# A mixture of experts on gathered token lists instead of all tokens, in a float32 two-block transformer kernel

## What is computed

```python
def moe(h, router_w, router_bias, w1, w3, w2):      # 16 experts, 4 groups of 4, D_EXPERT = 512
    scores = jax.nn.sigmoid(t.astype(f) @ router_w.astype(f))
    sel = scores + router_bias.astype(f)
    ...                                             # best group, then the top 2 experts inside it
    gate = ...                                      # (256, 16), two nonzero entries in each row
    for e in range(N_EXPERTS):
        hid = jax.nn.silu(t @ w1[e]) * (t @ w3[e])
        out = out + gate[:, e:e + 1] * (hid @ w2[e])
```

## Time and profile before

| | us |
|---|---|
| median of 3 runs | 1855.85 (1852.56 to 1878.67) |
| the profiled execution | 1855.94 |
| its span, first to last instruction | 1854.2 |
| w1(0) begins (end of the router's logits) | 622 |
| w2(0) ends | 672.7 |
| w2(14) ends, w3(15) begins | 1160.6 |
| last row of the experts' results added (L2320) | 1193.0 |

### The profile page before, as it was taken

How to read it: one execution, slowest core, us unless ns; L and a number is a source line. 1 busy time by engine, 2 the same in 40 slices (tenths; PEclk the granted TensorE clock), 3 DMA queues, 4 the chain that set the end, 5 groups by cost and what they waited for, 6 DMA issues and landing times.

```text
span 1854.2 us, 26650 instructions
## 1 busy us (share of the span) xinstructions
PE 1703.8 (92%) x11424; PEld 1485.0 (80%) x11424; DVE 1035.7 (56%) x1201; ACT 757.6 (41%) x851; POOL 191.4 (10%) x242
## 2 busy tenths in 40 slices
PE   4899988976797899999999999999999989999997
PEld 2678765765696798999999999777999977799996
DVE  1648356565666556555545555756555565655455
ACT  3433233622332343333333334454543365543444
POOL 0013551312320000610000000001000000000000
PEclk8999998976698899999999999999999999999999
DMA  9667500103336344555555555452555544245551
GB/s 351 239 246 242 111 28 1 24 10 81 90 125 219 113 171 166 188 183 183 190 182 182 182 182 182 144 182 76 182 183 191 194 159 162 99 161 196 188 182 68
DMA packets 150174, 289.15 MB, mean 156 GB/s; under 512 B 32439, under 2 KB 35646, under 8 KB 150057
## 3 DMA queue, kind: packets, MB, share of 16 engines
q1 hardware_dynamic: 135304, 270.50, 41.7%
q0 software_dynamic: 4816, 13.41, 2.4%
q10 hardware_dynamic: 9936, 3.54, 0.7%
HBM read 281.07 MB, written 6.37 MB: 155 GB/s over the span
## 4 chain that ended last, share of the span: by engine, by line
PE 77%; DVE 7%; issue 5%; ACT 4%; DMA 2%; DVEq 1%; SPq 1%; ACTq 1%; POOL 0%; POOLq 0%
PE psum L214 23%; PE psum L215 22%; PE psum L216 22%; DVE w_low L184 1%; DMA modw<-in_mod_w_dram 1%; DMA raw<-in_w_out_dram 1%; ACT w_high L179 1%; PE psum L748 1%; DVE w_low L202 1%; PE psum L3067 1%; PE psum L1537 1%; PE psum L765 1%; DVE blk L1173 1%; DVE outer L1170 1%; PE psum L3043 1%
## 5 line engine op out<-in xcount | busy, mean ns | idle before, releaser
L184 DVE TENSOR_TENSOR w_low<-raw,w_high 128x4096 fp32r<-128x4096 f32 x105 | 464.8, 4428 | 321.4 <-ACT w_high L179 319.5
L179 ACT ACTIVATE w_high<-raw 128x4096 fp32r<-128x4096 f32 x107 | 386.6, 3615 | 280.6 <-DMA raw<-in_moe_w_dram 142.5
L214 PE MATMUL psum<-act_high,w_high 128*128 128x256 f32 (+1 forms) x1176 | 337.2, 287 | 5.5 <-DVE w_low L184 5.5
L215 PE MATMUL psum<-act_low,w_high 128*128 128x256 f32 (+1 forms) x1176 | 336.4, 286 | 0.0
L216 PE MATMUL psum<-act_high,w_low 128*128 128x256 f32 (+1 forms) x1176 | 336.3, 286 | 0.0
L214 PEld LDWEIGHTS psum<-act_high,w_high 128*128 128x128 f32 x1176 | 227.6, 194 | 11.1 <-issue 9.6
L215 PEld LDWEIGHTS psum<-act_low,w_high 128*128 128x128 f32 x1176 | 227.5, 193 | 1.2
L216 PEld LDWEIGHTS psum<-act_high,w_low 128*128 128x128 f32 x1176 | 227.6, 194 | 0.7
L216 PE MATMUL psum<-actA_high,w_low 128*128 128x256 f32 x512 | 144.9, 283 | 0.0
L215 PE MATMUL psum<-actA_low,w_high 128*128 128x256 f32 x512 | 144.9, 283 | 0.0
L214 PE MATMUL psum<-actA_high,w_high 128*128 128x256 f32 x512 | 144.8, 283 | 0.0
(11 more groups left out here) (502 smaller groups left out, 3017.9 us busy)
## 6 DMA issues: line engine op xcount, KB each, us to landing
raw<-in_moe_w_dram SPq DMA_DIRECT2D x48, 2048.0 KB, 8.3
raw<-in_w_in_dram SPq DMA_DIRECT2D x20, 2048.0 KB, 8.9
raw<-in_w_up_dram SPq DMA_DIRECT2D x16, 2048.0 KB, 8.7
raw<-in_w_down_dram SPq DMA_DIRECT2D x16, 2048.0 KB, 7.8
modw<-in_mod_w_dram SPq DMA_DIRECT2D x12, 2048.0 KB, 12.8
raw<-in_w_out_dram SPq DMA_DIRECT2D x6, 2048.0 KB, 8.7
raw<-in_w_gate_dram SPq DMA_DIRECT2D x4, 2048.0 KB, 7.9
gates_d<-gstage ACTq DMA_DIRECT2D x8, 256.0 KB, 5.8
```

The costliest lines, as they stand in the source:

```text
L179: act.activation(WH[n % NSLOT][:, 0:elems], RAW[n % NSLOT][:, 0:elems], ACT.Copy).then_inc(s_wh, 1)
L184: dve.tensor_tensor(WL[n % NSLOT][:, 0:elems], RAW[n % NSLOT][:, 0:elems], WH[n % NSLOT][:, 0:elems].bitcast(F32), ALU.subtract).then_inc( ...
L214: pe.matmul(o, aH, wH, start=start, stop=False)
L215: pe.matmul(o, aH, wL, start=False, stop=False)
```

## The change

Experts 0 and 15 stay dense, on all 256 tokens. Experts 1 to 14 run on a list of at most 128 tokens each (128 slots). Three more passes (15, 16, 17) take the tokens past slot 128 of whatever experts are over-full; they always run, with weights fetched by row index. Pass 18 is expert 15. That makes 17 sparse and 2 dense passes in place of 16 dense ones. 57 panels are used instead of 48.

In a sparse pass the gathered tokens are the stationary operand and the panel's 512 columns are streamed: 24 matmuls of 512 columns for each of w1, w3 and w2. The hidden values come out by token, and are scaled by the gate of the slot, turned by 4 transposes (`hid_turn`), and split. The result of a pass, 128 x 1024, is copied out of PSUM by ACT and written to `y_rows` in DRAM by a DMA that ACT issues. The tokens of pass i+2 are gathered by an indirect DMA of POOL, turned by 8 transposes (`chosen_turn`) and split (`chosen_scalar`, `chosen_vector`).

Before the first sparse pass, DVE works out each token's two slots (`slots_vector`, 17 small instructions), from counts that TensorE makes (`positions_tensor`); POOL scatters token numbers and gates into `slots_d` (4 indirect DMAs), loads it back as `table`, and gathers. At the end POOL gathers each token's two result rows (4 indirect DMAs), adds them, and DVE multiplies and adds into `xres` (`pairs_vector`). Panels are handed to ACT, DVE and TensorE whole (`panel_half` waits for the whole panel). The small constants of this (`route_const_pool`) are made by POOL during the merge; `band` and `cmask` are made in passes 5 to 11. Renamed semaphores are left out of the diff.

```diff
+    def slots_vector(dve):
+        ...
+        dve.wait_ge(t_pos, n_pos + 1)
+        ...
+        dve.drain().then_inc(t_slot, 1)
+    def moe_pool(pool):
+        pool.wait_ge(t_slot, n_slot + 1)
+        pool.wait_ge(t_zero, n_zero + 32)
+        for q in range(2 * NT):
+            pool.indirect_dma_start(
+                out=slots_d[:, :], out_offset=bass.IndirectOffsetOnAxis(ap=slot_i[:, q:q + 1], axis=0),
+                in_=entry[:, q, :], in_offset=None).then_inc(t_out, 16)
+        pool.wait_ge(t_out, n_out + 32 * NT)
+        pool.dma_start(table[:, :, :], slots_d[0:REST, :].rearrange("(b s) c -> s b c", s=P)).then_inc(t_in, 16)
+        pool.wait_ge(t_in, n_in + 16)
+        pool.wait_ge(t_rows, n_rows + 16)
+        for i in range(1, LAST):
+            chosen_in(pool, i)
+            ...
+            if spills(i - 1):
+                spill_panel(pool, n_w3(i - 1), "moe_w3", i - 1)
+                spill_panel(pool, n_w1(i), "moe_w1", i)
+                spill_panel(pool, n_w2(i - 1), "moe_w2", i - 1)
+        ...
     def moe_scalar(act):
+        for i in range(1, LAST):
+            act.wait_ge(M["g"], i + 1)
+            act.activation(part_of(sg, i), psum[:, 0, :], ACT.Silu).then_inc(M["silu"], 1)
+            if i == 1:
+                chosen_scalar(act, 2)
+            split_high(act, n_w1(i + 1))
+            split_high(act, n_w2(i))
+            act.wait_ge(t_hT, n_hT + i)
+            act.activation(part_of(hidH, i), psum[:, 6, :], ACT.Copy).then_inc(M["hH2"], 1)
+            split_high(act, n_w3(i + 1))
+            act.wait_ge(s_wdone, n_w2(i) + 1)
+            if i >= 2:
+                act.wait_ge(t_yout, n_yout + 16 * (i - 1))
+            act.activation(ysb[:, :], psum[:, 4:6, :].rearrange("p b n -> p (b n)"), ACT.Copy).then_inc(t_y, 1)
+            act.wait_ge(t_y, n_y + i)
+            act.dma_start(y_rows[P * (i - 1):P * i, :], ysb[:, :]).then_inc(t_yout, 16)
+            if i + 2 < LAST:
+                chosen_scalar(act, i + 2)
     def moe_vector(dve):
+        for i in range(1, LAST):
+            split_low(dve, n_w1(i + 1))
+            dve.wait_ge(s_wdone, n_w3(i) + 1)
+            dve.wait_ge(M["silu"], i + 1)
+            dve.scalar_tensor_tensor(out=part_of(hidf, i), in0=psum[:, 1, :], scalar=table[:, i - 1, 1:2],
+                                     in1=part_of(sg, i), op0=ALU.mult, op1=ALU.mult).then_inc(M["hid"], 1)
+            dve.wait_ge(M["hH2"], i + 1)
+            dve.tensor_tensor(part_of(hidL, i), psum[:, 6, :], part_of(hidH, i).bitcast(F32), ALU.subtract
                               ).then_inc(M["hL2"], 1)
+            split_low(dve, n_w2(i))
+            split_low(dve, n_w3(i + 1))
+            if i + 2 < LAST:
+                chosen_vector(dve, i + 2)
     def moe_tensor(pe):
+        for i in range(1, LAST):
+            chosen_up(pe, 1, n_w3(i), i, 0)
+            chosen_up(pe, 1, n_w3(i), i, 1).then_inc(s_wdone, 1)
+            pe.wait_ge(M["silu"], i + 1)
+            if i + 1 < LAST:
+                pe.wait_ge(t_xL, n_xL + i + 1)
+                chosen_up(pe, 0, n_w1(i + 1), i + 1, 0)
+                hid_turn(pe, i)
+                chosen_up(pe, 0, n_w1(i + 1), i + 1, 1).then_inc(M["g"], 1)
+            ...
+            pe.drain().then_inc(s_wdone, 1)
+            chosen_down(pe, i)
+            if i + 2 < LAST:
+                chosen_turn(pe, i + 2)
```

More of the change, by code:

```diff
@@ L1821, in two_block_kernel @@
     gate = rtr.take("gate", [P, NT, E])
+    c2_end = free_off + 51 * KB + 512 + 13216
     scoT = rtr.take("scoT", [E, T])
-    n2st = stat[:, 64:80]
+    mem = rtr.take("mem", [P, NT, E])
+    slot = rtr.take("slot", [P, NT, E])
+    spill = rtr.take("spill", [P, NT, E - 2])
+    before = rtr.take("before", [P, E - 2, E - 2])
+    full = rtr.take("full", [P, E - 2])
+    nth_full = rtr.take("nth_full", [P, E - 2])
+    shift = rtr.take("shift", [P, E - 2])
+    own = Region(free_off + 51 * KB - 448, 960)
@@ new lines, in moe_sync, with chosen_in @@
+        load_panel(sp, n_w2(0), moe_src("moe_w2", 0))
+        load_panel(sp, n_w1(1), moe_src("moe_w1", 1))
+        for i in range(1, NS):
+            if not spills(i):
+                load_panel(sp, n_w3(i), moe_src("moe_w3", i))
+            if i < LAST and not spills(i + 1):
+                load_panel(sp, n_w1(i + 1), moe_src("moe_w1", i + 1))
+            if not spills(i):
+                load_panel(sp, n_w2(i), moe_src("moe_w2", i))
+    def chosen_in(pool, i):
+        if i >= 2:
+            pool.wait_ge(t_xT, n_xT + i - 1)
+        pool.indirect_dma_start(
+            out=chosen[:, :], out_offset=None, in_=h_rows[:, :],
+            in_offset=bass.IndirectOffsetOnAxis(ap=table[:, i - 1, 0:1].bitcast(I32), axis=0)
+        ).then_inc(t_chosen, 16)
@@ L2286, in moe_vector @@
         dve.drain()
-        dve.wait_ge(M["silu"], E)
+        split_low(dve, n_w2(LAST))
+        dve.wait_ge(M["silu"], NS)
         for b in range(2):
@@ L2299, in moe_vector @@
         dve.wait_ge(B["gcol"], 1)
+        pairs_vector(dve, 0)
         last_vector(dve, 0, 0)
@@ L2304, in moe_vector @@
         turn_vector(dve, 0, 0, 0, 1)
+        pairs_vector(dve, 1)
         last_vector(dve, 1, 0)
@@ new lines, in positions_tensor @@
+    def positions_tensor(pe):
+        pe.wait_ge(t_mem, n_mem + 1)
+        pe.wait_ge(t_const, n_const + 1)
+        o = psum[:, 6, 64:64 + (NT + 1) * E].rearrange("p (t e) -> p t e", e=E)
+        for t in range(NT):
+            pe.matmul(o[:, t, :], earlier[:, :], mem[:, t, :], start=True, stop=t == 0)
+            if t:
+                pe.matmul(o[:, t, :], ones[:, :], mem[:, 0, :], start=False, stop=True)
+        for t in range(NT):
+            m = pe.matmul(o[:, NT, :], ones[:, :], mem[:, t, :], start=t == 0, stop=t == NT - 1)
+        m.then_inc(t_pos, 1)
```

535 lines of the change are left out of this document (382 added, 153 removed).

## The result

| | before | changed |
|---|---|---|
| median | 1854.2 us (4 runs) | 1908.8 us (4 runs, 1904.6 to 1913.3) |
| ratio to before | | 1.026, 95% interval 1.018 to 1.035 |
| profiled execution, span | 1854.2 us | 1911.5 us |
| mean granted clock of it | 0.951 | 0.900 |

The changed kernel is slower by 2.6%. The interval runs from 1.8% to 3.5%: the loss is sure, that it is over 2% only likely.

What follows compares the result with a forecast made beforehand. It took TensorE's matmul stream to bound the kernel before, and a serial chain of copies plus clock falls after. Terms +20.8, +2.5, +4 and +2 made +29.3 on 1854.2, so 1885 us forecast; range 1829 to 1922.

Steps and rivals of the forecast that it cites:

- the sum: Whole kernel: +20.8 + 2.5 + 4 + 2 = +29.3 us on a span of 1854.2 us, giving 1883.5.
- What bounds after the change: Sparse passes: the serial chain through the engines' in-order lists, 26.0 us a pass at full clock, TensorE idle twice.
- The forecast chain: One pass, from w1's first matmul: w2 starts at 9.24 us, the next w1 at 26.07, each step awaiting the last.
- The clock: Both TensorE waits of a pass: falls to 1.2 GHz cost 1.75 us each, making the pass 29.5 us.
- clock stays high: Rival: no fall in one or both waits of a pass, 28 us less for each, 1857 or 1829 us; chance 0.23.
- longer stretches: Rival: low clock costs 2.7 us at each wait, pass 31.4 us, +30 us, 1915 us; chance 0.20.
- The start: Before the first sparse pass: slots, scatters, table, gather and transposes let w1(1) start at 671 us, bounds 666 and 681.
- Constants and overflow panels: Pass 1's reciprocal with its minima, +2.5 us; the nine spill panels fetched through POOL, +2 us (0 to 15).
- 20.8: Start and passes: w2(17) ends at 1181.4 us where w2(14) ended at 1160.6 before, +20.8 us.
- The end: After the last list: gathers, additions and write, about 19 us, hidden under 23 us of expert 15; `pairs_vector` adds +4.
- The second block: Stage after the experts: the forecast had no term for it.
- the forecast's count: TensorE in the expert passes: 17 sparse passes would take 306 us where the 14 rounds take 488.

Runs made afterwards that it cites:

- e4_two_passes_less: Changed kernel with two of its three overflow passes left out: 1857.9 us, distance from hid to hid 30.12 us.
- e7_block2_and_sum: Changed kernel with token-pair sums on VectorE and identity turns in idle times of the second block's attention stage, both layers: 1900.6 us.
- e12_three_halves_filled: e11_three_halves plus 3 filler matmuls ahead of hid's turn and 6 behind it: ratio 0.955 to the kernel before, 1770 to 1775 us in three of six executions.
- e5_hid_first: Changed kernel reordered: hid made before w1's low part, turned before w1, copied before w2's high part: 1852.1 us, distance 26.25 us.
- e9_halves: Changed kernel with w1 and w2 panels split and handed over in two halves: 1851.4 us, distance 25.34 us.
- e11_three_halves: e10 with w3's panel also split and handed over in two halves: 1781.3 us, ratio 0.961 to the kernel before.
- e10: Changed kernel with the edits of e5_hid_first, e9_halves and e7_block2_and_sum together: 1807.7 us, ratio 0.974 to the kernel before.

## Why the prediction came out as it did

The time lay in the range given, 1829 to 1922, and the sign of the forecast was right; 24 us of the 55 were missing, and the forecast's own narrower range, 1865 to 1900, was passed. That the time lies in the range is owed to its width: over half of the missing time came from a stage that the sum does not have. By its own steps:

- **What bounds after the change: right.** The forecast chain has w2 at 9.24 us and w1 at 26.07 us behind the start of w1; at full clock a pass measured 26.12. TensorE's two idle times were put at 4.6 and 3.1 us and are 4.78 and 3.08. Each handoff named is in the rows above, in that order.
- **The clock: right that it falls at both waits in every pass, term too small.** Twice 1.75 was 3.5 us; w1 lost 2.2 and w2 1.9 in the mean, filling the waits gave back 3.9, and the changed kernel ran at 30.06 us where 29.5 was forecast, 9 us over the 16 distances. The rival "clock stays high" fell; 30.06 lies between my value and the 31.4 us of "longer stretches". The Trainium skill ("TensorE: Matmul & The Clock Gate", HAM oscillation in real kernels) describes a fall in every tile where the wait is longer than the tile's matmuls. Here the waits, 4.8 and 3.1 us, were shorter than the 15 and 7.5 us of matmuls ahead of them, and the clock fell all the same, behind both waits of every pass.
- **The start: right in sum, not in its parts.** The slots stood at 643.5, as forecast once it is allowed for that the front of this trace is 3.8 us earlier (both choices stand at 636.4 and not at 640.2). w1(1) began at 668.3 where 671 - 3.8 = 667.2 was forecast. The four scatters took 10.1 us to the table's load (7 forecast), the table 4.5 (7.5), the gather 6.5 (5).
- **Constants and overflow panels: one small, one too large.** The first two distances were 4.7 and 1.8 us over the rest; +2.5 was forecast for the reciprocal. The overflow passes cost nothing over others (e4_two_passes_less), +2 was forecast. With the clock these make w2 of the last list end 32.7 us later than before, where 20.8 + 2.5 + 2 = 25.3 was the sum. That the difference is only 7.4 is in part luck: the front was 3.8 us earlier, which no term had.
- **The end: mis-sized, +10.3 instead of +4.** Write, four gathers and a sum were put at about 19 us and hidden under expert 15. From the last copy of a list's result (1193.6) to the first sum used (1219.4) they took 25.8: 9.0 to the write's landing, 6.2 to issue the gathers, 8.1 to their landing, 2.5 for the sum. The step that failed is the durations. They came from transfers of the kernel before; here two panels of the next stage were loading at the same time (11.2 us to landing), but whether that is what made these longer was not tried.
- **The second block: not in the sum at all, +14.4.** This is the largest miss. I had looked at idle times only where the change made them. The stage has idle times of 0.95 us in the kernel before as well, and the clock stood there; in the changed kernel it fell in the same stage at the same idle time, in both layers (7 us each). e7_block2_and_sum and the four other variants with its turns show that it was this, and that 13 short turns in each layer prevent it.

7.4 + 6.3 + 14.4 = 28.1 us is the difference between +29.3 and +57.3 in the spans.

That the change is no gain although it takes 182 us of TensorE's work away (488 - 306, the forecast's count) has thus two named reasons: the matmuls were the cover of 24 us of copies, and a path of short pieces with idle times between them runs at the lower clock. Both could be mended without touching what is computed (e12_three_halves_filled, some 135 us less than the changed kernel).

Open: why the one pass in which the panels change from SyncE's queue to GpSimd's is 30 us long in e12_three_halves_filled and 35.9 in e5_hid_first. A high part waits 8.4 us for a landing there, in a kernel whose loads land in 10.4 in the median; whether it is the queues' order or the indirect transfers' rate was not tried.

## What to carry to other kernels

When the work that covers the copies is cut, list the copies in the order of each engine's list before anything else: the new time is the chain through them, and an instruction of 0.7 us behind one of 4.4 (hid behind w1's low part) was part of an order that cost 4.5 us of 30. Hand large operands over in parts once nothing covers the hand-over; here halves were worth 4.7 us of 30. Count the clock with every idle time, over many passes and not from one, also in stages that the change does not touch, and give idle TensorE harmless work only where it stands in front of nothing.

## What the hardware showed that I had not expected

- The same code with the same idle time, and two outcomes. Ahead of the probabilities' turn in the attention stage TensorE was idle 0.95 us before, 0.94 in the changed kernel and 0.94 in e9_halves, which does not touch this stage; the clock behind it was 1.00, 0.50 and 1.00, and from the last addition to the end e9_halves took 662.2 us. In e11_three_halves too, idle times of 0.85 and 1.63 us ahead of w1 were followed by either. The idle time next to a fall does not decide it alone; what else does is not settled here. The rows of the kernel before, of the changed one and of e9_halves, TensorE's timelines, and the stretch behind the last:

```profile
1264.33 0.66 PE L3053 MATMUL psum<-ident,prob 128*128 128x128 f32 x4 [0.95 <-ACTq L2622]
...
1307.16 1.11 PE L3408 MATMUL psum<-ident,prob 128*128 128x128 f32 x4 [0.94 <-ACTq L2977]
...
1259.46 0.66 PE L3430 MATMUL psum<-ident,prob 128*128 128x128 f32 x4 [0.94 <-ACTq L2999]
```

```profile
1263.00:1268.00 5.00, 4.32 (x31) 3.57 (x31) 3.41 (x9) 1.84 (x6) 0.00 (x0) 1.00 0.00 0
```

- A 2 MB panel took 8.3 us from issue to landing in the kernel before, and 9.7, 10.6, 9.9, 10.8 and 10.8 (medians of 800 to 1000 us) in the changed kernel, e5, e10, e11 and e12, which moved 247, 285, 303, 320 and 343 GB/s there. A sum for a faster loop that takes its load from the kernel before comes out 1.4 to 2.5 us short.
- Issuing an indirect DMA holds GpSimd for 0.94 to 1.07 us where no VectorE low part runs beside it. Nine of these issues in the changed kernel begin while the low part of a panel runs. They take 2.2 to 5.15 us, and every one of them ends 0.8 to 0.9 us behind the end of the low part. GpSimd's timeline, the fourth scatter and an overflow panel, and VectorE's beside the latter:

```profile
646.33 1.59 POOL L2423 DMA_INDIRECT slots_d<-entry,slot_i  x1 [0.30 <-issue]
648.22 4.03 POOL L2423 DMA_INDIRECT slots_d<-entry,slot_i  x1 [0.31 <-issue]
...
1109.84 5.15 POOL L2389 DMA_INDIRECT raw<-in_moe_w_dram,spill_i  x1 [4.15 <-PE psum L229]
```

```profile
1109.74 4.42 DVE L197 TENSOR_TENSOR w_low<-raw,w_high 128x4096 fp32r<-128x4096 f32 x1 [2.78 <-ACT w_high L192]
```

The low part beside the fourth scatter runs from 647.0 to 651.4, and the scatter's issue ends at 652.3. This fits the Trainium skill's statement on the shared port pair ("SBUF — State Buffer", SBUF: two separate sides), that GpSimd's reads wait for a VectorE instruction with two inputs in SBUF. In the start it met the fourth scatter in full, and this is the 3 us by which the scatters were longer than forecast. The overflow panels, whose issues were held up for longer, cost their passes nothing (e4_two_passes_less).
